# Second pass of a chunked scan: the two directions' decay matrices summed on VectorE before one product per pair of heads

## What is computed

```python
def chunked_scan(q, k, v, log_a, include_diag):      # chunks of 128 positions
    ...
    def step(h, inp):
        qq, kk, vv, aa = inp
        cs = jnp.cumsum(aa, axis=1)
        seg = cs[:, :, None] - cs[:, None, :]
        decay = jnp.exp(jnp.where(mask[None, :, :, None, None], seg, -jnp.inf))
        qk = jnp.einsum('bjgn,blgn->bjlg', qq, kk)
        y_intra = jnp.einsum('bjlgh,blghp->bjghp', qk[..., None] * decay, vv)
        y_inter = jnp.einsum('bjgn,bghnp->bjghp', qq, h) * jnp.exp(cs)[..., None]
        ...

def bidir_scan(q, k, v_f, v_b, a_f, a_b):
    y_f = chunked_scan(q, k, v_f, a_f, True)
    flip = lambda t: jnp.flip(t, axis=1)
    y_b = flip(chunked_scan(flip(q), flip(k), flip(v_b), flip(a_b), False))
    return y_f + y_b
```

## Time and profile before

| | us |
|---|---|
| median of 3 runs | 1842.67 (1841.26 to 1842.90) |
| the profiled execution | 1842.35 |
| its span, first to last instruction | 1840.5 |
| PE busy | 1765.4 (96%) |
| DVE busy | 1152.8 (63%) |
| ACT busy | 773.1 (42%) |
| POOL busy | 174.9 (10%) |
| mean granted clock of PE | 0.986 of full speed |

### The profile page before, as it was taken

How to read it: one execution, slowest core, us unless ns; L and a number is a source line. 1 busy time by engine, 2 the same in 40 slices (tenths; PEclk the granted TensorE clock), 3 DMA queues, 4 the chain that set the end, 5 groups by cost and what they waited for, 6 DMA issues and landing times.

```text
span 1840.5 us, 20756 instructions
## 1 busy us (share of the span) xinstructions
PE 1765.4 (96%) x8246; PEld 1376.2 (75%) x8246; DVE 1152.8 (63%) x1553; ACT 773.1 (42%) x1302; POOL 174.9 (10%) x200
## 2 busy tenths in 40 slices
PE   9999988899999999999999899999989999999996
PEld 6777757677667888888877687776668788888885
DVE  4553645686766788664346998676765568766333
ACT  4443543453233454443223454655463345444320
POOL 0311000230000011110000000112220001111000
PEclk9999999999999999999999999999999999999998
DMA  5211201421112223233322222111102233232331
GB/s 213 80 58 46 81 23 70 148 80 58 58 46 92 92 94 101 93 99 101 94 89 75 81 92 69 35 35 46 35 24 92 69 104 102 92 103 89 96 101 58
DMA packets 42752, 147.88 MB, mean 80 GB/s; under 512 B 5152, under 2 KB 6304, under 8 KB 42528
## 3 DMA queue, kind: packets, MB, share of 16 engines
q1 hardware_dynamic: 39168, 138.43, 23.2%
q10 hardware_dynamic: 3488, 8.12, 1.3%
HBM read 144.44 MB, written 2.10 MB: 80 GB/s over the span
## 4 chain that ended last, share of the span: by engine, by line
PE 81%; DVE 12%; ACT 4%; issue 1%; DMA 1%; ACTq 0%; POOL 0%; DVEq 0%
PE bank L347 23%; PE bank L349 22%; PE bank L348 22%; DVE cv L1794 4%; DVE w_lo L311 2%; PE bank L1177 2%; PE bank L1895 1%; PE bank L1856 1%; PE bank L1868 1%; PE bank L693 1%; PE bank L706 1%; DVE bank L523 1%; ACT w_hi L304 1%; PE bank L1877 1%; PE bank L1886 1%
## 5 line engine op out<-in xcount | busy, mean ns | idle before, releaser
L347 PE MATMUL bank<-a_hi,w_hi 128*128 128x512 f32 x1504 | 607.3, 404 | 19.0 <-DVE cv L1794 6.7
L311 DVE TENSOR_TENSOR w_lo<-raw,w_hi 128x1024 fp32r<-128x1024 f32 (+1 forms) x264 | 335.6, 1274 | 443.6 <-ACT w_hi L304 443.0
L348 PE MATMUL bank<-a_lo,w_hi 128*128 128x512 f32 x1504 | 590.0, 392 | 0.0
L349 PE MATMUL bank<-a_hi,w_lo 128*128 128x512 f32 x1504 | 589.7, 392 | 0.0
L304 ACT ACTIVATE w_hi<-raw 128x1024 fp32r<-128x1024 f32 (+1 forms) x264 | 274.1, 1042 | 384.9 <-DMA raw<-in_w_down 142.3
L347 PEld LDWEIGHTS bank<-a_hi,w_hi 128*128 128x128 f32 x1504 | 285.1, 190 | 102.3 <-issue 28.4
L348 PEld LDWEIGHTS bank<-a_lo,w_hi 128*128 128x128 f32 x1504 | 285.1, 190 | 64.7 <-issue 7.2
L349 PEld LDWEIGHTS bank<-a_hi,w_lo 128*128 128x128 f32 x1504 | 284.8, 189 | 60.7
L1055 ACT ACTIVATE u<-bank,par 128x512 f32<-128x512 f32 x88 | 68.6, 780 | 176.3 <-DVE bank L523 176.3
L347 PE MATMUL bank<-g_hi,w_hi 128*128 128x512 f32 x352 | 136.9, 389 | 0.0
L348 PE MATMUL bank<-g_lo,w_hi 128*128 128x512 f32 x352 | 136.9, 389 | 0.0
(11 more groups left out here) (356 smaller groups left out, 2055.5 us busy)
## 6 DMA issues: line engine op xcount, KB each, us to landing
raw<-in_w_up SPq DMA_DIRECT2D x88, 512.0 KB, 3.6
raw<-in_w_in SPq DMA_DIRECT2D x52, 512.0 KB, 3.7
raw<-in_w_out SPq DMA_DIRECT2D x32, 512.0 KB, 3.7
raw<-in_w_down SPq DMA_DIRECT2D x32, 512.0 KB, 3.5
raw<-in_w_xbc SPq DMA_DIRECT2D x24, 512.0 KB, 3.6
raw<-in_w_z SPq DMA_DIRECT2D x16, 512.0 KB, 3.7
raw<-in_w_down SPq DMA_DIRECT2D x16, 384.0 KB, 3.1
x<-in_xT ACTq DMA_DIRECT2D x4, 512.0 KB, 7.1
```

The source lines that it names most:

```text
L311: nc.vector.tensor_tensor(w_lo[:, q % RING, 0:w], raw[:, q % RING, 0:w], w_hi[:, q % RING, 0:w].bitcast(F32), ALU.subtract).then_inc(lo_do ...
L347: nc.tensor.matmul(out, wh, rhs_hi[:, k, :], start=k == first, stop=False)
L348: nc.tensor.matmul(out, wh, rhs_lo[:, k, :], start=False, stop=False)
L349: return nc.tensor.matmul(out, wl, rhs_hi[:, k, :], start=False, stop=stop)
```

## The change

The places of both directions are added on DVE (`joined`), the sum is multiplied by `gmat` into a new buffer `emc` of two places (`weigh`, now once per pair of heads), and `inside` runs once per pair, after the next pair's first spreads. `emc` lies on the memory of `vtl`, so the first `weigh` of a group waits for the last of the states (`stp`), and the others for the pass before (`intra`). ACT no longer waits for `intra` but for `mlu`: a place of `em` is free when the product of its head is made. The PE loop has four rounds instead of eight, and the steps on DVE that stood between single `weigh` stand behind pairs.

```diff
@@ -213,6 +213,7 @@
     gmat = at("gmat", [P, S], ST + 89)
     ident_r = at("ident_r", [P, P], ST + 91, F32R)
     vtl = at("vtl", [P, 2, GW], ST + 95)
+    emc = at("emc", [P, 2, S], ST + 95)
     btok = at("btok", [P, TT, NS], ST + 99)
     nrm_a = at("nrm_a", [P, S], ST + 101)
     em = at("em", [P, 4, S], 56)
@@ -1886,16 +1887,20 @@
                 nc.tensor.matmul(bank[2 + i % 2][:, c * P:(c + 1) * P], y12[:, c, i * P:(i + 1) * P], C["ident"],
                                  start=c == 0, stop=False, skip_group_check=True)
 
-        def inside(g, m):
-            i, d = m // 2, m % 2
-            pe.wait_ge(mlu, STEPS * g + 2 * m + 2)
+        def inside(g, i):
+            pe.wait_ge(mlu, 8 * g + 2 * i + 2)
             for c in range(TT):
                 for hh in range(2):
-                    n = 2 * m + hh
                     mm = nc.tensor.matmul(bank[2 + i % 2][hh * HD:(hh + 1) * HD, c * P:(c + 1) * P],
-                                          xtok[:, c, (2 * i + hh) * HD:(2 * i + hh + 1) * HD], em[:, n % 4, c * P:(c + 1) * P],
-                                          start=False, stop=d == 1 and c == TT - 1, skip_group_check=True)
+                                          xtok[:, c, (2 * i + hh) * HD:(2 * i + hh + 1) * HD], emc[:, hh, c * P:(c + 1) * P],
+                                          start=False, stop=c == TT - 1, skip_group_check=True)
             mm.then_inc(intra, 1)
+
+        def fill(g, ks):
+            if g == SG - 1:
+                for k in ks:
+                    out3_step(pe, 0, k)
+                    out3_step(pe, 1, k)
 
         def norm_sum(g):
             pe.wait_ge(yadd, 3 * (g + 1))
@@ -1931,29 +1936,24 @@
             if g + 1 < SG:
                 for q in range(4):
                     part_z(4 * g + 4, q)
-            for m in range(8):
-                if m < 7:
-                    spread(g, 2 * m + 2)
-                    spread(g, 2 * m + 3)
+            for i in range(4):
+                spread(g, 4 * i + 2)
+                spread(g, 4 * i + 3)
+                if i:
+                    inside(g, i - 1)
+                carried(g, i)
+                if g + 1 < SG:
+                    part_z(4 * g + 5, i)
+                if i < 3:
+                    fill(g, (2 * i,))
+                    spread(g, 4 * i + 4)
+                    spread(g, 4 * i + 5)
+                    fill(g, (2 * i + 1,))
                 else:
                     if g + 1 < SG:
                         begin(g + 1)
-                if m % 2 == 0:
-                    carried(g, m // 2)
-                if m % 2 and g + 1 < SG:
-                    part_z(4 * g + 5, m // 2)
-                inside(g, m)
-                if g == SG - 1:
-                    if 1 <= m < 6:
-                        out3_step(pe, 0, m - 1)
-                        out3_step(pe, 1, m - 1)
-                    if m == 6:
-                        for k in (5, 6):
-                            out3_step(pe, 0, k)
-                            out3_step(pe, 1, k)
-                    if m == 7:
-                        out3_step(pe, 0, 7)
-                        out3_step(pe, 1, 7)
+                    fill(g, (6, 7))
+            inside(g, 3)
 
     def out3_step(pe, t, k):
         pe.wait_ge(ylo, k + 1)
@@ -2005,7 +2005,7 @@
             h = HPG * g + 2 * i + hh
             act.wait_ge(xp, STEPS * g + n + 1)
             if n >= 4:
-                act.wait_ge(intra, 8 * g + n // 2 - 1)
+                act.wait_ge(mlu, 8 * g + 2 * (i - 1) + hh + 1)
             for c in range(TT):
                 e = nc.scalar.activation(em[:, n % 4, c * P:(c + 1) * P], bank[4 + n % 2][:, c * P:(c + 1) * P], ACT.Exp,
                                          bias=lbias[:, c, d, h:h + 1])
@@ -2020,7 +2020,7 @@
             for n, c in enumerate(XT_ORDER):
                 act.wait_ge(txp, TT * g + n + 1)
                 if n == 0 and g:
-                    act.wait_ge(intra, 8 * g)
+                    act.wait_ge(intra, 4 * g)
                 nc.scalar.activation(xtok[:, c, :], bank[4 + n % 2][:, :], ACT.Copy).then_inc(xtc, 1)
             if g:
                 squares(g - 1, 0)
@@ -2124,7 +2124,7 @@
                 into = c if s != 1 else (3 if d == 0 else 0)
                 dve.wait_ge(inter, 6 * g + 2 * s + d + 1)
                 if s == 0 and g:
-                    dve.wait_ge(intra, 8 * g)
+                    dve.wait_ge(intra, 4 * g)
                 nc.vector.tensor_tensor(wide(y12[:, into, :]), wide(bank[2 + d][:, :]), heads(cume, c, d, g), ALU.mult).then_inc(comb, 1)
                 if s == 1:
                     dve.wait_ge(comb, 6 * g + 2 * s + d + 1)
@@ -2140,18 +2140,25 @@
         def masks(g):
             dve.wait_ge(gp, g + 1)
             if g:
-                dve.wait_ge(mlu, STEPS * g)
+                dve.wait_ge(mlu, 8 * g)
             nc.vector.tensor_copy(gmat[:, :], bank[7][:, :]).then_inc(gl_done, 1)
 
-        def weigh(g, n):
-            dve.wait_ge(e_x, STEPS * g + n + 1)
-            if n == 0:
+        def joined(g, i, hh):
+            dve.wait_ge(e_x, STEPS * g + 4 * i + hh + 3)
+            return nc.vector.tensor_tensor(em[:, hh, :], em[:, hh, :], em[:, 2 + hh, :], ALU.add)
+
+        def weigh(g, i):
+            if i == 0:
                 dve.wait_ge(gl_done, g + 1)
-            nc.vector.tensor_tensor(em[:, n % 4, :], em[:, n % 4, :], gmat[:, :], ALU.mult).then_inc(mlu, 1)
+                dve.wait_ge(stp, 6 * (g + 1))
+            else:
+                dve.wait_ge(intra, 4 * g + i)
+            for hh in range(2):
+                nc.vector.tensor_tensor(emc[:, hh, :], em[:, hh, :], gmat[:, :], ALU.mult).then_inc(mlu, 1)
 
         def evac_y(g, i):
             k = 4 * g + i
-            dve.wait_ge(intra, 8 * g + 2 * i + 2)
+            dve.wait_ge(intra, 4 * g + i + 1)
             nc.vector.scalar_tensor_tensor(out=xbc[:, k, :], in0=xbc[:, k, :], scalar=pcol("d_skip", k), in1=bank[2 + i % 2][:, :],
                                            op0=ALU.mult, op1=ALU.add).then_inc(yev, 1)
 
@@ -2184,19 +2191,11 @@
             nc.vector.scalar_tensor_tensor(out=xbc[:, k, :], in0=xbc[:, k, :], scalar=pcol("ssd_g", k), in1=xbc[:, B_TILE + g, :],
                                            op0=ALU.mult, op1=ALU.mult).then_inc(yn, 1)
 
-        def last_step(n):
-            if 1 <= n < 4:
-                low(n - 1)
-            if n == 8:
-                low(3)
+        def last_step(i):
+            for k in ((2, 3), (4,), (5, 6, 7), (8, 9, 10))[i]:
+                low(k)
+            if i == 1:
                 lo_to(dve, z0 + 4 * SG + 4)
-            if 10 <= n < 14:
-                low(n - 6)
-            if n == 14:
-                low(8)
-            if n == 15:
-                low(9)
-                low(10)
 
         def low(k):
             dve.wait_ge(yhi, k + 1)
@@ -2218,24 +2217,28 @@
             fed(g, 2)
             take_z(4 * g + 3)
             carry(g, 2)
-            for n in range(STEPS):
-                weigh(g, n)
-                if n in (5, 9, 13):
-                    evac_y(g, n // 4 - 1)
-                if n == 4 and g:
+            if g == SG - 1:
+                low(0)
+                low(1)
+            for i in range(4):
+                joined(g, i, 0)
+                link("dve", dve, joined(g, i, 1))
+                weigh(g, i)
+                if g and i == 0:
                     root_half(g - 1)
-                if n == 5 and g:
                     root_first(g - 1)
-                if n == 6 and g:
+                if g and i == 1:
                     root_second(g - 1)
-                if n == 7 and g:
                     root_third(g - 1)
-                if 9 <= n < 13 and g:
-                    normed_y(g - 1, n - 9)
-                if n == 11 and g + 1 < SG:
+                if i:
+                    evac_y(g, i - 1)
+                if g and i == 2:
+                    for n in range(4):
+                        normed_y(g - 1, n)
+                if i == 2 and g + 1 < SG:
                     take_z(4 * g + 4)
                 if g == SG - 1:
-                    last_step(n)
+                    last_step(i)
             evac_y(g, 3)
             if g + 1 < SG:
                 take_z(4 * g + 5)
```

## The result

Four runs of the changed kernel gave 1858.66 us (1857.39 to 1860.03), four of the one before beside them 1842.76: a ratio of 1.0089, 95% interval 1.0074 to 1.0104. It is slower, by 15.9 us where 11.9 were forecast. The profiled execution took 1858.79 us, its span is 1857.1 (before 1840.5).

A forecast was written before the change was run, and what follows sets the result against it. PE's own work was taken to bound groups 0 to 2, and what PE waits for the last group. Terms of 3.9, 5.6 and 2.4 sum to 11.9 us on 1842.35: 1854.2 us, range 1845 to 1860.

The forecast's parts named there:

- the two waits of four spreads in a row: Groups 0 to 2: four spreads (decay matmul pairs) share two banks, so PE waits for ACT 0.91 and 0.46 us a round.
- The weight split: Groups 0 to 2: ACT's split behind step 8, formerly hidden by PE's work, now makes PE wait 0.95 us for step 9.
- Groups 0 to 2 together: +3.9 us: First three groups: +3.0 us from PE's waits less saved passes, +0.9 from POOL and DVE; bounds +1 and +7.
- forecast +1.0: Each of groups 0 to 2: 5.05 us of added waits less 4.08 us of removed passes on PE.
- the +0.9 of POOL and DVE at the turn of a group: Late silu(z) products on POOL run beside DVE's weight split and delay the next group's first `tailed`: 0.45 us in two groups.
- The last group: +5.6 forecast: PE waits 4.0 us for `low(5)` ahead of spread 14, then half clock; the sum of squares (line 1973) comes 5.6 us later.
- The first rival: The last group stays even because ACT and DVE have `low(5)` in time: only +3.9, 1846.3 us; chance 0.15.
- Behind the sum of squares: +2.4 forecast: After PE waits about 4.7 us at line 1973, its clock is lost again, adding 2.4 us behind it.
- "DVE is not the limit": Groups 0 to 2: ACT's four steps and DVE make 5.8 us against PE's round of 6.95, about 1 us to spare.
- The faster rival: Spreads don't hold PE if ACT finishes each step before PE arrives: 16.3 us come off, 1826 us; chance 0.06.
- The rival of full blocking: Every DVE overlap with POOL blocks in full: four products of 1.66 on the last group's chain, 1858.6 us; chance 0.10.
- two stretches of 1.08: Last group: DVE work stretched 1.08 us under a POOL product, once before `low(5)` ends, once before `evac_y(3)`.

The follow-up runs named there:

- z_between: The changed kernel with the z quarter put between spreads 4i+5 and 4i+6 on PE: 1847.42 us, 1.0028 of before.
- split_later: The changed kernel with ACT's weight split moved from behind step 8 to behind step 11, except in the last group: 1852.38 us, 1.0054 of before.
- dummies: The changed kernel with useless matmuls on PE where it waits (three behind spread 4i+5, four between spreads 10 and 11): 1854.82 us, 1.0071 of before.
- fill_late: The changed kernel with step 5 of the output projection issued behind spread 15 instead of ahead of spread 14: 1854.45 us, 1.0059 of before.
- best_warm: best with useless matmuls in two PE pauses, ahead of the last group's spread 2 and of the sum of squares: 1833.05 us, 0.9951 of before.
- dve_spread: The changed kernel with only DVE's order altered: last group's low splits 5 to 7 earlier, ssd_g products spread over rounds: 1853.28 us, 1.0057 of before.
- old_order: The changed kernel with PE's eight half rounds of two spreads back, one pass per pair at the odd ones: 1848.05 us, 1.0031 of before.
- no_sum: old_order without the sums of the two directions on DVE, so one direction's decays are missing from the result: 1834.87 us, 0.9960 of before.
- best: old_order's PE loop and the change's sums, with weight splits, ssd_g products and last-group steps shared out anew on DVE and ACT: 1834.45 us, 0.9959 of before.

## Why the prediction was right, and where its terms were off

The direction, the range and the mechanisms held; some terms were mis-sized, and part of the sum came out by luck.

**Right: the two waits of four spreads in a row.** Forecast 0.91 and 0.46. The profile shows 0.81 and 0.30, but counts idle time from the end of the record before (0.39 us), where the forecast counted from the time the next matmul could have started (0.23); counted as in the forecast they are 0.97 and 0.46. The round was forecast at 6.95 and measured 7.01. The weight split: with it 7.90 was forecast, and 9.49 less the 1.58 of clock is 7.91. z_between takes the waits between the spreads down and split_later the one for the split, and the time goes.

**Mis-sized: "Groups 0 to 2 together: +3.9 us".** It was +7.5, a little past the upper bound of +7. What the sum lacked is the clock. I let a pause cost more than itself only where it was as long as the 3.83 and 4.61 us of the earlier trace rows, and counted waits of 0.8 to 1.4 us at their own length. Yet behind 0.77 and 1.25 us, close together and after a round with waits, the clock was 0.51. With 1.6 on the forecast +1.0 group 0 comes to +2.6, and +2.60 was measured; dummies gives 1.6, 1.34 and 1.32 back. These 4.3 are nearly all of the 4.5 by which the three groups exceed the forecast 3 x 1.0; the +0.9 below, which did not come, hid a part of it.

**Not seen: the +0.9 of POOL and DVE at the turn of a group.** The first matmul of group 1's chunk states, for which PE needs the first `tailed`, starts 3.94 us behind the first one of `turn_x`, and before it was 3.95. Two other things that the sum left out nearly cancel. In groups 1 and 2 the first spread that waits does so for 1.97 us instead of 0.8: ACT makes the roots of the group before (lines 1992 and 1994) between steps 1 and 2, so sums and product come later, and step 4 waits for the product. Before, the last pass of each of these groups waited 1.0 us for VectorE, which is now gone.

```profile
1222.38 0.74 ACT L1992 ACTIVATE xbc<-bank,eps_col 128x512 f32<-128x512 f32 x1
1223.15 0.63 ACT L1994 ACTIVATE xbc<-xbc 128x512 f32<-128x512 f32 x1
1223.69 2.17 ACT L2010 ACTIVATE em<-bank,lbias 128x128 f32<-128x128 f32 x8
```

**The last group: +5.6 forecast, +5.11 measured.** The chain that was named holds: `low(5)` behind sums, products and ssd_g products, then step 14, then POOL; fill_late gives 3.0 back. But its total is nearer than its terms. The way from spread 2 to spread 12 was not even but 24.66 us (from 1344.77 to 1369.43) for 23.33, and again the clock is what was missing: from the second pass (1364.43) to spread 12 PE takes 5.00 us, mostly at half clock, where the same work from the first pass on, 1355.58 to 1358.99, takes 3.41. VectorE did not wait for that, so the wait on `fill(5)` was 3.05 us (3.2 counted as in the forecast) instead of 4.0, and from spread 12 to the sum of squares it is 23.40 for 19.62, +3.8 instead of +5.6. And the clock behind the long wait came later than forecast: the six matmuls of `fill(5)` still ran at full clock (0.39 us), and the half clock fell on spreads 14 and 15 and the pass.

**The range held, with some luck.** The sum of 11.9 for a measured 15.9 lacks the clock of groups 0 to 2 (4.3) and has 0.9 for POOL and DVE that did not come, so that one error hid a part of the other. +7.5 lies outside the forecast's own bound of +7 for these groups, and 1858.66 is 1.3 us inside the upper end of the range. The first rival, a last group that stays even, is out with the +5.1.

**Behind the sum of squares: +2.4 forecast, +2.94 measured,** after a wait for POOL of 3.55 (4.7 forecast, 3.7 when counted as there); best_warm takes 1.6 of such a loss away.

**"DVE is not the limit"** was right for the change (dve_spread), and only just: in the order that does not hold PE up it is the limit (old_order, no_sum). The faster rival had this as its blind spot: it took only ACT's durations as the condition, and with the spreads' waits shortened the time was 1847 to 1848, not 1826 (z_between, old_order).

**The rival of full blocking** gave 1858.6, the measured time to 0.1, which is luck. Its mechanism is right and its sizes are wrong. A POOL product that meets no work on DVE takes 1.27 us; the 1.66 that the forecast took for a product alone is one that had itself waited for a DVE instruction already under way. And a DVE product held by POOL ends 0.55 us behind POOL's end, whenever it began:

```profile
1235.90 1.27 POOL L2082 TENSOR_TENSOR xbc<-xbc,zt 128x512 f32<-128x512 f32 x1 [33.48 <-DVE xbc L2162]
...
1369.34 1.72 POOL L2082 TENSOR_TENSOR xbc<-xbc,zt 128x512 f32<-128x512 f32 x1 [5.49 <-DVE xbc L2162]
1369.84 1.77 DVE L2191 SCALAR_TENSOR_TENSOR xbc<-xbc,par 128x512 f32<-128x512 f32 x1
...
1382.18 1.66 POOL L2082 TENSOR_TENSOR xbc<-xbc,zt 128x512 f32<-128x512 f32 x1 [11.13 <-DVE xbc L2162]
1382.62 1.77 DVE L2202 TENSOR_TENSOR y_lo<-xbc,y_hi 128x512 fp32r<-128x512 f32 x1
```

POOL ends at 1371.06 and 1383.84, DVE at 1371.61 and 1384.39; the stretched product of before does the same (1361.53 and 1362.08, and the earlier trace rows). So DVE is held until POOL is through, and loses what was left of POOL's product when it came, at most 1.1 us here. On the path from spread 12 to the sum of squares that happened twice: four ssd_g products took 3.75 us for 2.73, and three low splits 2.97 for 1.88, 2.1 us in place of the rival's 6.6 and near the forecast's two stretches of 1.08. The Trainium skill (SBUF — State Buffer, "Who interferes with whom") has whichever of the two issues first hold the shared ports for its whole instruction, while the other fully blocks. These rows agree with it, in both directions.

## What to carry to other kernels

Half the passes on the busiest engine are worth what its next wait leaves of them: before ordering four producers in a row over two buffers, count the consumer's time per buffer against the work that stood between them. When a trace shows an engine that must be kept fed, price each new wait at its length plus the lower clock that several of them bring. In this kernel, adding work to a second engine to spare the first paid only once the second engine's steps were shared out between the new products (best against old_order), so plan both orders together.
